# Wide and small expert places spread in groups of five, and an earlier second half of a wide split

## The reference, cut to what matters

```python
gates = softmax(top_val)                    # 512 tokens, 4 of 32 experts each
for each expert e, for each block of its tokens:
    gu   = x_block @ mlp1_w[e] + mlp1_b[e]  # 1024 x 2048 weights, float32
    gate, up = gu[..., ::2], gu[..., 1::2]
    act  = (clip(up, -7, 7) + 1) * min(gate, 7) * sigmoid(1.702 * min(gate, 7))
    y    = act @ mlp2_w[e] + mlp2_b[e]      # 1024 x 1024 weights, float32
    out[token] += gate_of(token, e) * y
```

## Time and profile before

| | us |
|---|---|
| median of three runs | 1551.12 |
| lowest and highest | 1547.3, 1551.7 |
| the profiled execution, its own time | 1548.36 |
| span of its trace | 1546.7 |
| the loop over places, from the bias of place 3 to that of place 31 | 919.3 |

### The profile page before, as it was taken

One profiled execution on the slowest core, in us unless ns is written; L12 is line 12 of the kernel. 1 busy time (PEld: TensorE's weight loads), 2 busy tenths in 40 slices (PEclk: granted clock), 3 DMA queues, 4 the chain that ended last, 5 costly groups with the idle time before them and its releaser, 6 DMA issues.

```text
span 1546.7 us, 25543 instructions
## 1 busy us (share of the span) xinstructions
PE 1445.5 (93%) x9333; PEld 1073.6 (69%) x9334; DVE 1229.2 (79%) x1068; ACT 1015.3 (66%) x997; POOL 425.0 (27%) x253
## 2 busy tenths in 40 slices
PE   6999999996989999999999999999999999999885
PEld 5777777775867686777767777776777767655554
DVE  5556656565379799998999989899998989888984
ACT  4635353525256577787877878877787777677763
POOL 7100000000018421443324334243342325122210
PEclk8999999997979999999999999999999999999987
DMA  6211111004379899999999999999999999999991
GB/s 203 66 56 43 43 50 48 18 15 179 139 278 378 313 401 398 409 410 393 409 394 413 397 392 411 391 413 392 391 419 386 388 392 383 388 388 396 401 372 77
DMA packets 96942, 457.47 MB, mean 296 GB/s; under 512 B 11199, under 2 KB 37999, under 8 KB 47585
## 3 DMA queue, kind: packets, MB, share of 16 engines
q1 hardware_dynamic: 86176, 429.63, 69.3%
q0 software_dynamic: 10688, 26.80, 6.3%
HBM read 443.57 MB, written 18.10 MB: 298 GB/s over the span
## 4 chain that ended last, share of the span: by engine, by line
PE 40%; DMA 13%; issue 9%; DVE 7%; ACT 4%; POOL 1%; SPq 1%; DVEq 0%; ACTq 0%; POOLq 0%
PE psum L2179 12%; DMA w_pieces<-in_mlp_w 12%; PE psum L2182 6%; PE psum L2200 4%; PE psum L2250 3%; DVE w_pieces_lo L1943 3%; ACT w_pieces_hi L1743 3%; PE psum L2255 3%; PE psum L1387 3%; PE psum L2192 2%; PE psum L2189 2%; PE psum L2223 1%; DVE xl L1983 1%; DVE silu L1956 1%; POOL slot_lists L1685 1%
## 5 line engine op out<-in xcount | busy, mean ns | idle before, releaser
L1943 DVE TENSOR_TENSOR w_pieces_lo<-w_pieces,w_pieces_hi 128x2048 fp32r<-128x2048 f32 x346 | 784.0, 2282 | 104.4 <-ACT w_pieces_hi L1743 103.0
L1743 ACT ACTIVATE w_pieces_hi<-w_pieces 128x2048 fp32r<-128x2048 f32 x346 | 661.7, 1915 | 244.4 <-DMA w_pieces<-in_mlp_w 146.4
L1676 POOL DMA_INDIRECT sum_rows<-ys,this_i x30 | 211.1, 7036 | 359.3 <-ACT ys L1795 196.7
L2250 PE MATMUL psum<-w_pieces_hi,ah 128*128 128x512 f32 x512 | 148.1, 394 | 6.7 <-DVE ah L1952 6.3
L2255 PE MATMUL psum<-w_pieces_lo,ah 128*128 128x512 f32 x512 | 139.5, 395 | 8.0 <-DVE w_pieces_lo L1943 8.0
L2179 PE MATMUL psum<-w_pieces_hi,xh 128*128 128x512 f32 x440 | 123.7, 403 | 14.4 <-DVE xl L1983 14.4
L2200 PE MATMUL psum<-w_pieces,x_native 128*64 128x512 f32 x288 | 133.0, 605 | 0.0
L2189 PE MATMUL psum<-w_pieces_hi,xh 128*128 128x512 f32 x432 | 124.8, 411 | 3.4 <-ACT w_pieces_hi L1743 3.4
L2192 PE MATMUL psum<-w_pieces_lo,xh 128*128 128x512 f32 x432 | 119.1, 398 | 7.6 <-DVE w_pieces_lo L1943 7.6
L2179 PE MATMUL psum<-w_pieces_hi,xl 128*128 128x512 f32 x440 | 118.1, 390 | 0.0
L2182 PE MATMUL psum<-w_pieces_lo,xh 128*128 128x512 f32 x440 | 117.9, 390 | 0.0
(11 more groups left out here) (421 smaller groups left out, 2186.5 us busy)
## 6 DMA issues: line engine op xcount, KB each, us to landing
w_pieces<-in_mlp_w SPq DMA_DIRECT2D x384, 1024.0 KB, 9.9
w_raw<-in_w_in SPq DMA_DIRECT2D x26, 512.0 KB, 4.1
w_pieces<-in_w_out SPq DMA_DIRECT2D x8, 512.0 KB, 9.3
chunk_work<-in_x SPq DMA_DIRECT2D x4, 512.0 KB, 6.6
sc<-pall POOLq DMA_DIRECT2D x16, 128.0 KB, 4.6
x<-in_x SPq DMA_DIRECT2D x4, 512.0 KB, 13.7
sum_rows<-x POOLq DMA_DIRECT2D x4, 512.0 KB, 3.3
h_rows<-w_pieces POOLq DMA_DIRECT2D x4, 512.0 KB, 2.9
```

The costliest lines, as they stand in the source:

```text
L1676: nc.gpsimd.indirect_dma_start(sum_dram, bass.IndirectOffsetOnAxis(this_i[rows, 0:1], 0), ys[rows, :], None, bounds_check=S - 1, oob_is_er ...
L1743: nc.scalar.activation(hi[:, p % RING], raw[:, raw_slot(b, p)].rearrange("p r n -> p (r n)"), ACT.Copy).then_inc(s_hi, done)
L1943: nc.vector.tensor_tensor(lo[:, p % RING], raw[:, raw_slot(b, p)].rearrange("p r n -> p (r n)"), hi[:, p % RING].bitcast(F32), ALU.subtrac ...
L2250: nc.tensor.matmul(bank(into + c), a[:, 2 * p + r2, :], hi[:, p % RING, r2 * D + c * 512:r2 * D + (c + 1) * 512], start=p == 0 and r2 == 0 ...
```

## The change

1. The places are dealt in groups of five from place 2 on: wide, small, wide, small, small, six times. There are still fourteen wide and eighteen small places, and places 0 and 1 are still wide.
2. `over_loop` writes out the first group (places 2 to 6) and runs a hardware loop of five iterations over the other five groups. The numbers that semaphores are waited for follow the place (`small_done`, `small_step`) in place of a count of small places.
3. Place 2 is wide now. Its gather, its bias rows, its turn and its selection are the wide forms.
4. GpSimd loads the slot lists in nine DMAs in place of six, since the places stand in five strides.
5. The second half of a wide place's row split (`x_hi(.., 1)`, `x_lo(.., 1)`) stands behind piece 3, ahead of the clip on VectorE and of the activation on ScalarE, in place of behind piece 4.

```diff
-MIXED = (4, 26)
-WIDE_PLACES = (0, 1) + tuple(range(3, MIXED[1], 2))
-SMALL_PLACES = tuple(e for e in range(EXPERTS) if e not in WIDE_PLACES)
+GROUP = 5
+SMALL_AT = (1, 3, 4)
+STEP = {1: 2, 3: 2, 4: 1}
+SMALL_PLACES = tuple(e for e in range(2, EXPERTS) if (e - 2) % GROUP in SMALL_AT)
+WIDE_PLACES = tuple(e for e in range(EXPERTS) if e not in SMALL_PLACES)
...
     def over_loop(eng, steady, r):
-        for b in range(2, MIXED[0]):
-            steady(r, b, None)
-        with eng.Fori(MIXED[0], MIXED[1], 2) as b:
-            steady(r, b, "even")
-            steady(r, b + 1, "odd")
-        for b in range(MIXED[1], MIXED[1] + 2):
-            steady(r, b, None)
-        with eng.Fori(MIXED[1] + 2, EXPERTS) as b:
-            steady(r, b, "tail")
+        for b in range(2, 2 + GROUP):
+            steady(r, b, b - 2)
+        with eng.Fori(2 + GROUP, EXPERTS - GROUP + 1, GROUP) as b:
+            for part in range(GROUP):
+                steady(r, b + part, part)
...
-            for places in (slice(0, 2), slice(3, MIXED[1], 2)):
+            for places in wide_slices:
                 nc.gpsimd.dma_start(lists[:, places, :], rows[bass.ds(r * P, P), places, :]).then_inc(s_lists, 16)
-            for places in (slice(2, MIXED[1], 2), slice(MIXED[1], EXPERTS)):
+            for places in small_slices:
                 for half in (top_half, low_half):
...
                 if p == 3 and up_small:
                     x_small(r, b)
+                if p == 3 and not up_small:
+                    x_lo(r, b, 1)
                 if p == 3 and act_small:
-                    clip_small(r, b - 1)
-                if p == 4 and not up_small:
-                    x_lo(r, b, 1)
+                    clip_small(r, b - 1, part - 1)
```

More of the change, by code:

```diff
@@ L1541, in small, with small_done, small_step @@
             return b + ahead in SMALL_PLACES
[L1542 to L1550, removed]
+        return (part + ahead) % GROUP in SMALL_AT
+    def small_done(r, e):
+        return r * (2 * (EXPERTS - 2)) + (e * 2 - 2)
+    def small_step(part):
+        return 2 * STEP[part % GROUP]
     def made(p, natives=NATIVE):
@@ L1699, in run @@
             rows = g["list_dram"].rearrange("(s e) w -> s e w", e=EXPERTS)
-            for places in (slice(0, 2), slice(3, MIXED[1], 2)):
+            wide_slices = [slice(0, 2)] + [slice(2 + at, EXPERTS, GROUP) for at in range(GROUP) if at not in SMALL_AT]
+            small_slices = [slice(2 + at, EXPERTS, GROUP) for at in SMALL_AT]
+            for places in wide_slices:
                 nc.gpsimd.dma_start(lists[:, places, :], rows[bass.ds(r * P, P), places, :]).then_inc(s_lists, 16)
-            for places in (slice(2, MIXED[1], 2), slice(MIXED[1], EXPERTS)):
+            for places in small_slices:
                 for half in (top_half, low_half):
                     nc.gpsimd.dma_start(lists[half, places, :], rows[bass.ds(r * HALF, HALF), places, :]).then_inc(s_lists, 16)
-            pool.wait_ge(s_lists, r * 96 + 96)
+            loads = len(wide_slices) + 2 * len(small_slices)
+            pool.wait_ge(s_lists, (r * loads + loads) * 16)
             pool.sem_inc(s_part, 1)
@@ L1757, in a_small, with move_low @@
             nc.scalar.activation(ah[:, :, 0:HALF], halves(bank(from_bank)), ACT.Copy).then_inc(s_ah, 2)
-        def move_low(r, e, b, p):
+        def move_low(r, e, b, p, part):
             act.wait_ge(s_used, r * STREAM + (place(b, p) + 1 + RING))
@@ L1762, in move_low, with y_small @@
             act.wait_ge(s_y, r * EXPERTS + e)
-            nc.scalar.activation(sg[top_half, :], pairs(e)[low_half, :, 0], ACT.Copy).then_inc(s_low, 1)
+            nc.scalar.activation(sg[top_half, :], pairs(e)[low_half, :, 0], ACT.Copy).then_inc(s_low, small_step(part) - 1)
             nc.scalar.activation(uu[top_half, :], pairs(e)[low_half, :, 1], ACT.Copy).then_inc(s_low, 1)
-        def y_small(r, e, b):
+        def y_small(r, e, b, part):
             act.wait_ge(s_used, r * STREAM + (place(b, DOWN - 1) + 1 + RING))
@@ L1769, in y_small @@
             act.wait_ge(s_act, r * EXPERTS + (e + 3))
-            nc.scalar.activation(sg[top_half, :], psum[low_half, 0:2, :].rearrange("p b n -> p (b n)"), ACT.Copy, scale=this_g[low_half, 0:1]).then_inc(s_ylow, 2)
+            nc.scalar.activation(sg[top_half, :], psum[low_half, 0:2, :].rearrange("p b n -> p (b n)"), ACT.Copy, scale=this_g[low_half, 0:1]).then_inc(s_ylow, small_step(part))
         def x_whole(r, m, q, from_bank):
@@ L1818, in steady @@
                 if p == 3 and act_small:
-                    move_low(r, b - 1, b - 1, PIECES - 1)
+                    move_low(r, b - 1, b - 1, PIECES - 1, part - 1)
                 if not (up_small and p in NATIVE):
@@ L1825, in steady @@
                     x_small(r, b)
+                if p == 3 and not up_small:
+                    x_hi(r, b, 1)
                 if p == 3 and act_small:
-                    silu_small(r, b - 1, part)
-                if p == 4 and not up_small:
-                    x_hi(r, b, 1)
+                    silu_small(r, b - 1)
                 if p == 4 and not act_small:
@@ L1833, in steady @@
                     if down_small:
-                        y_small(r, b - 2, b)
+                        y_small(r, b - 2, b, part - 2)
                     else:
@@ L1968, in activate_small, with add_y @@
             nc.vector.scalar_tensor_tensor(av[top_half, :], sg[top_half, :], SILU_MAX, uu[top_half, :], ALU.min, ALU.mult).then_inc(s_act, 1)
[L1970 to L1971 removed]
+        def add_y(r, e):
+            dve.wait_ge(s_ylow, small_done(r, e))
             dve.wait_ge(s_stored, r * SCATTERED + (e + 1))
@@ L2006, in steady @@
                     if act_small:
-                        add_halves(r, b - 1, part)
+                        add_halves(r, b - 1, part - 1)
                     else:
@@ L2012, in steady @@
                 if p == 7 and down_small:
-                    add_y(r, b - 2, part)
+                    add_y(r, b - 2)
                 if p == 1 and not up_small:
@@ L2017, in steady @@
                     x_small(r, b)
+                if p == 3 and not up_small:
+                    x_lo(r, b, 1)
                 if p == 3 and act_small:
-                    clip_small(r, b - 1)
-                if p == 4 and not up_small:
-                    x_lo(r, b, 1)
+                    clip_small(r, b - 1, part - 1)
                 if p == 4:
                     if act_small:
-                        activate_small(r, b - 1, part)
+                        activate_small(r, b - 1)
                     else:
```

43 lines of the change are left out of this document (21 added, 22 removed).

## The result

| | before | after |
|---|---|---|
| median | 1547.74 | 1553.23 |
| lowest to highest | 1544.7 to 1552.78 | 1547.65 to 1560.25 |
| executions | 22 | 22 |
| profiled execution | 1548.36 | 1558.61 |
| bias of place 3 | 548.02 | 553.35 |

The ratio is 1.0034, interval 1.0023 to 1.0044: slower by 5.5 us, just above what a measurement of this kernel can tell from no change. The forecast was 1545.4 against a median of 1551.12, 5.7 us faster. A second batch of the very same kernel gave 1.0014 (0.9996 to 1.0032), 3.2 us between the medians; the two intervals overlap from 1.0023 to 1.0032.

A forecast was written before the change was run, and what follows sets the result against it. It took TensorE and transfers as level in the alternating pairs (64.25 and 64.20 us), and transfers plus dips as the bound of the small places at the end. -9.1 + 1.3 + 2.1 = -5.7 us gave 1545.4, range 1537 to 1555.

The forecast's parts named there:

- The dips behind wide places (-9.1 us): Small places behind wide ones: an earlier TensorE frees slots sooner and closes transfer dips, -9.1 us, bounds 0 and -15.1.
- the six tenths: Small places behind wide ones: the part taken of at most 12 x 1.26 = 15.1 us of dips that closes.
- 64.20 us a pair: Alternating part of the loop: the time in which transfers could carry a wide and a small place, against TensorE's 64.25.
- a group would take 161 us: Loop: sign that the forecast is right, a group of five places in about 161 us; 163.5 or more means wrong.
- The gap of 1.21 us at "cost nothing": Ahead of a wide place: the earlier row split closes TensorE's 1.21 us wait for `xl`, at no cost elsewhere.
- Small behind small (+1.3 us): Loop: six small places behind small ones where five stood, so one more dip, +1.3 us, bounds 0 and +1.5.
- Start-up (+2.1, bounds 0 and 5.0): Before place 3: three more list loads delay `this_g` by +2.1 us; 5.0 if TensorE's extra work also counts.
- start-up pays: Rival, places 0 to 2: three wide places load TensorE, +2.1 + 2.9 us, dips stay, +1.3: 1557.4; chance 0.10.
- slack of 2 us per group: Loop: per group of five, TensorE needs 157.76 us and transfers 159.73, leaving TensorE 2 us to catch up.
- dips stay: Rival, loop: the closed gap turns into waits for data; 1551.1 to 1554.5, put at 1552.5; chance 0.28.
- Code loading: Rival, hardware loop: the longer body doesn't stay resident, so jumps back cost 3.5 to 18 us; 1556 or more; chance 0.05.
- ScalarE's wait near 11.6 us: Place 2: sign that the forecast is right, ScalarE's wait for `this_g` near 11.6 us, where before it was 9.48.

The follow-up runs named there:

- the early split alone: Before, with only the second half of a wide place's row split moved behind piece 3: 1545.88 against 1547.82, ratio 0.9994.
- the two other traces of its loop code: Before with nine list loads (ratio 0.9997), and before with place 0's scaling at place 2 behind piece 11 in place of 7 (ratio 0.9987).
- the kernel with the small place first: After, with groups ordered small wide wide small small, so place 2 is small; nine list loads kept: 1595.99 against before's 1547.82, ratio 1.0199.

## Why the prediction was wrong, step by step

**The dips behind wide places (-9.1 us): the step that failed most.** TensorE did come out of the wide place 1 us earlier, but the six tenths that I took were a quarter in the measured case: transfer idle there went from 0.93 to 0.67 us in the early split alone, which over twelve places is 3 us in place of 9.1. Of a pair 0.26 us arrived (65.75 to 65.49 on average), of the loop nothing (919.30 to 919.67), and the median moved by -1.9 us, within noise. After has 0.67 too. The reason lies one step before: I read a share of 1.02 as what transfers can do in every stretch, and got 64.20 us a pair. The early split's pair moves 410 and 399 GB/s, a mean of 404.5, where before moved 403; the share rose from 0.98 to 1.00 in the small place and fell from 1.02 to 1.01 in the wide one. What looked like a dip was in part the same bytes in another place, as the near equal GB/s of the pairs suggest. Nor is 1.02 the reading without gaps: the stretch from 515 to 520 reads 1.04. The forecast that a group would take 161 us went with this term: 165.6 and 164.0 in the two traces, above the 163.5 that I had named as the sign of dips that stay.

**The gap of 1.21 us at "cost nothing".** Right: no such wait is left, and in before's pairs the edit harms nothing (0.9994). "What is late next: the data" was right too, only sooner than in the sum.

**Small behind small (+1.3 us).** The mechanism was right, the size too small. I had priced one more such place, not that each takes longer. The average one took 32.95 us in before (33.25 and 33.52 in the two other traces of its loop code), and 34.19 and 34.13 in the two traces of after, five of them each: 5 x 0.6 to 1.2 = 3 to 6 us on top of the place more. Of two of them (982.94 above; one at 1146.95) the granted clock is 0.95. Other stretches gave part of that back, wide behind small above all, 33.52 to 32.71 and 32.46 us, so that the loop in sum is +1 us by the estimate above. How much of the 3 to 6 us is the clock and how much waiting stays open.

**Start-up (+2.1, bounds 0 and 5.0).** Measured +4.8 by the estimate above, near the upper bound, and the cause was wrong. I put the 0.71 us of a list load on the path; three more cost nothing (0.9997; lists at 520.17). And I named the wide place 2 as a help, since its slots come free earlier. It was the harm: +3.19 us of TensorE's work and +2.83 us of its idle time, less 0.69 by which the stretch began earlier, is +5.33 at the bias of place 3. With place 2 small it is at 546.1. The sign that I gave for this case ("more than 3 us later than 548.0") showed: 5.3 and 4.2.

**The sum by what was measured.** +4.8 for start-up and +1 for the loop are 5.8; the medians differ by 5.5. That the two agree is partly luck, since single traces of one loop differ by up to 8.6 us, and no run had the groups with a short start-up and an undisturbed loop. What is shown is that the -9.1 us didn't come and that the wide place 2 lengthens its own stretch by 5 to 6 us; that this is what the median lost is an estimate. The rival *start-up pays* had this mechanism ("TensorE, not the loads, is still behind when place 3 begins"), with 2.9 us for the extra work (3.19 measured), and was given 0.10, too little: I weighed the slack of 2 us per group against it, but that slack is TensorE's, and my reading, not tested, is that the loads which start-up loses are what the loop lacks. The rival *dips stay* had the dips right, which for the most part stayed, and start-up too small: its sum is +1.3 to +3.4 us (1552.4 to 1554.5, where the text begins at 1551.1), and +5.5 were measured.

**Code loading.** Not seen: 54 instruction packets against 51, and none between 840 and 1480 us, which is from the second iteration of the loop to its end. The trace agrees with what the prediction cites from the Trainium skill ("Runtime: NRT & Kernel Launch", Instruction fetch mechanics): TensorE's 3793 matmuls and 3792 weight loads of 28 places make, as an estimate, some 1350 in a body of five, under the 2048 given there.

**ScalarE's wait near 11.6 us.** 14.23 us, and 15.0 in the second batch's trace, by the later landing, not the issue.

## What to carry to other kernels

A DMA share above that of the neighbours is not a capacity: before a dip is priced, take the bytes per second over the whole period, since filling a dip may only move bytes. Cost a small load at start-up by when it lands among the large ones, not by its issue, and ask what an earlier free slot puts in front of it. Where the median of one kernel moves by a few us, take two traces of it before assigning a difference to a stretch: here the loop of one and the same kernel took 916 and 925 us. And where an edit is tried on the changed kernel, lay its stretch beside that of the kernel before with the same edit.

## What the runs showed of the hardware that I had not expected

**VectorE holds GpSimd's issue of an indirect DMA.** Already in before a scatter, issued in 1.9 to 4.8 us where VectorE has gaps, takes 13.59 us while VectorE works without one. It ends at 763.56, 1.5 us behind VectorE's first idle moment of 0.19 us:

```profile
749.97 13.59 POOL L1676 DMA_INDIRECT sum_rows<-ys,this_i  x1 [14.83 <-ACT ys L1795]
```
```profile
757.62 4.47 DVE L1943 TENSOR_TENSOR w_pieces_lo<-w_pieces,w_pieces_hi 128x2048 fp32r<-128x2048 f32 x2
762.28 2.29 DVE L1943 TENSOR_TENSOR w_pieces_lo<-w_pieces,w_pieces_hi 128x2048 fp32r<-128x2048 f32 x1 [0.19 <-ACT w_pieces_hi L1743]
```

In after the same takes 16.3 to 18.4 us in seven of the scatters, in the kernel with the small place first a gather takes up to 31.4. A split reads two operands from SBUF. The Trainium skill (GPSIMD Engine Reference, Key points) says that GpSimd shares its SBUF interfaces with VectorE and contends with VectorE's instructions that have two SBUF inputs; the trace agrees, though no run separates the splits from VectorE's other work. Waits of VectorE for its own split, three in a wide place, bring all issues in the loop under 4.9 us; they were worth 46 us where gathers were held (from 1595.99 to 1552.49, in two batches) and nothing in after, where nearly all that was held were scatters.

**A short wait of TensorE and the clock.** Behind waits of 1.2 to 2.2 us inside dense work some places have a mean granted clock of 0.91 to 0.95, which is a few us at 1.2 in place of 2.4 GHz. The wide ones take 33.5 to 35.9 us where 32.5 is usual at 1.00. But the wait alone doesn't decide: in after, waits of 2.11 us (before the matmul at 684.13) and 2.42 us (739.34) were followed by places at 1.00. What else it takes stays open; no run varied it alone.
